# Stage borders of a two-block transformer kernel: row block 1 runs three tiles behind, splits and norms take another order

## The reference

```
first_block:                                   # once
    mixer: attention + hyena convolution + Fourier mixing, gated, w_out;  x = x + g1 * y
    x = x + g2 * expert_choice_moe(h2, ...)    # 16 experts, each takes 32 tokens
    return rms_norm(x, final_g)
second_block:  for i in range(2):              # two layers
    f = swiglu(rmsnorm(h, g[0]), gate[i,0], up[i,0], down[i,0]);  h = h + 0.5 * rmsnorm(f, g[1])
    mix = hybrid_mixer(rmsnorm(h, g[2]), rope tables, ...)        # latent + dilated attention
    h = h + rmsnorm(mix, g[3])
    f = swiglu(rmsnorm(h, g[4]), gate[i,1], up[i,1], down[i,1]);  h = h + 0.5 * rmsnorm(f, g[5])
    gate = sigmoid(rmsnorm(h, g[6]) @ w_ple_gate[i])
    h = h + rmsnorm((p[i] @ w_ple[i]) * gate, g[7])
```

## Time and profile before

| | |
|---|---|
| median of 3 runs | 2546.86 us (2542.1 to 2547.43) |
| profiled execution, time | 2549.01 us |
| profiled execution, span | 2547.7 us, mean granted clock 0.886 |
| TensorE busy | 2082.2 us (82%) |
| VectorE busy | 930.4 us (37%) |
| ScalarE busy | 603.8 us (24%) |
| memory read | 644.48 MB, mean 253 GB/s |

### The profile page before, as it was taken

The page is one execution under the profiler, slowest core; times in us unless marked ns, Lnnn a source line. Parts: engine busy times, 40 slices in busy tenths (PEclk is TensorE's granted clock), DMA queues, the critical chain, the costliest instruction groups (busy, mean ns, idle before and its releaser), DMA issues.

```text
span 2547.7 us, 28159 instructions
## 1 busy us (share of the span) xinstructions
PE 2082.2 (82%) x11876; PEld 1366.9 (54%) x11876; DVE 930.4 (37%) x1195; ACT 603.8 (24%) x744; POOL 68.8 (3%) x147
## 2 busy tenths in 40 slices
PE   6899998766666666666667999889997999889997
PEld 3556675211111111111115998678996998668995
DVE  1531323100000000000004666756656566756655
ACT  2121011000000000000002444344434444344443
POOL 0000000000000000000000000000001000000001
PEclk9898997977877777778787999989998999989998
DMA  7224454999999999999995554325553555305551
GB/s 304 102 106 179 167 215 184 425 424 425 425 424 425 424 425 425 424 425 425 424 425 233 190 187 139 120 77 180 191 188 118 179 193 176 120 33 191 192 192 64
DMA packets 93254, 647.37 MB, mean 254 GB/s; under 512 B 11495, under 2 KB 12424, under 8 KB 16328
## 3 DMA queue, kind: packets, MB, share of 16 engines
q1 hardware_dynamic: 89856, 639.93, 63.6%
q10 hardware_dynamic: 3272, 5.64, 0.6%
HBM read 644.48 MB, written 1.05 MB: 253 GB/s over the span
## 4 chain that ended last, share of the span: by engine, by line
PE 50%; DMA 33%; DVE 11%; ACT 3%; issue 2%; POOL 1%; SPq 1%; ACTq 0%; DVEq 0%; POOLq 0%
PE PS L812 10%; PE PS L814 10%; PE PS L813 10%; DMA ring<-in_md 9%; DMA ring<-in_mu 8%; PE PS L395 4%; DVE low L1589 3%; DMA XT<-in_mu 2%; DMA XT<-in_md 2%; PE PS L784 2%; PE PS L753 1%; DMA tables<-in_mu 1%; DMA QT<-in_mu 1%; DMA c_dft<-in_mu 1%; ACT WH L1942 1%
## 5 line engine op out<-in xcount | busy, mean ns | idle before, releaser
L1589 DVE TENSOR_TENSOR low<-ring,WH 128x2048 fp32r<-128x2048 f32 (+1 forms) x164 | 374.4, 2283 | 186.0 <-ACT WH L1942 183.4
L812 PE MATMUL PS<-XH,WH 128*128 128x256 f32 x1408 | 400.4, 284 | 17.0 <-DVE XL L1607 13.7
L813 PE MATMUL PS<-XL,WH 128*128 128x256 f32 x1408 | 399.1, 283 | 0.0
L814 PE MATMUL PS<-XH,low 128*128 128x256 f32 x1408 | 397.4, 282 | 0.0
L1942 ACT ACTIVATE WH<-ring 128x2048 fp32r<-128x2048 f32 (+1 forms) x164 | 313.0, 1909 | 33.2 <-PE PS L792 26.8
L812 PEld LDWEIGHTS PS<-XH,WH 128*128 128x128 f32 x1408 | 269.0, 191 | 19.6 <-issue 14.4
L814 PEld LDWEIGHTS PS<-XH,low 128*128 128x128 f32 x1408 | 271.4, 193 | 0.0
L813 PEld LDWEIGHTS PS<-XL,WH 128*128 128x128 f32 x1408 | 268.7, 191 | 1.4
L1571 DVE TENSOR_TENSOR SS<-SS,PS 128x512 f32<-128x512 f32 x16 | 11.0, 688 | 553.5 <-PE PS L753 553.5
L753 PE MATMUL PS<-ring,big 128*32 128x512 f32 x928 | 151.2, 752 | 74.8 <-DMA ring<-in_mu 45.2
L784 PE MATMUL PS<-ring,PT 128*32 128x512 f32 x480 | 98.4, 850 | 63.2 <-DMA ring<-in_md 53.0
(11 more groups left out here) (381 smaller groups left out, 2570.1 us busy)
## 6 DMA issues: line engine op xcount, KB each, us to landing
ring<-in_mu SPq DMA_DIRECT2D x62, 1024.0 KB, 26.6
ring<-in_md SPq DMA_DIRECT2D x60, 1024.0 KB, 26.7
ring<-in_mg SPq DMA_DIRECT2D x54, 1024.0 KB, 26.5
ring<-in_fg SPq DMA_DIRECT2D x44, 1024.0 KB, 4.8
ring<-in_fu SPq DMA_DIRECT2D x44, 1024.0 KB, 4.8
ring<-in_fd SPq DMA_DIRECT2D x44, 1024.0 KB, 4.8
ring<-in_wmod SPq DMA_DIRECT2D x24, 1024.0 KB, 6.9
XT<-in_mg SPq DMA_DIRECT2D x21, 1024.0 KB, 26.7
```

The costliest lines, as they stand in the source:

```text
L812: t.matmul(o, l[0], r[0], start=start, stop=False, skip_group_check=True)
L813: t.matmul(o, l[0], r[1], start=False, stop=False, skip_group_check=True)
L814: return t.matmul(o, l[1], r[0], start=False, stop=stop, skip_group_check=True)
L1589: own(v.tensor_tensor(low[:, w.slot.index, 0:size], w.flat, WH[:, w.slot.index, 0:size].bitcast(f32), ALU.subtract).then_inc(*c.wl.up()), ...
```

## The change

Eight parts:

1. *Entry.* The residual is added on TensorE: after expert 2, four identity matmuls add `XR` into the scatter banks. At the end VectorE and ScalarE copy two halves each. The splits of the first two tiles stand ahead of this, the third after the first gains. The loads of tiles 2 and 3 go ahead of the load of the gain row.
2. *Turn-overs* in expert 15: four identity matmuls after each of the 16 gate and up tiles, six after each of three down steps.
3. *Rope tables* made in block one, after the first affines; `pos` and `invs` are loaded early.
4. *Feed-forward end.* Down projections of tiles 8, 9 and 10 for m = 0, then 8 and 9 for m = 1, transposes of m = 0, then 10 for m = 1. The ring order of the tiles follows.
5. *Events 4l+1 and 4l+3.* Splits, norms, factors and gains of the two m take another order on VectorE, ScalarE and GpSimd; transposes of m = 1 lie between two halves of a weight block. The gate's sigmoid table is loaded early; event 4 of layer 0 handles m = 0 inside the gate's last block.
6. *Heads.* `latent_heads` alternates keys and queries; the second dilated rotation follows all copies on VectorE.
7. *Attention.* ScalarE copies probabilities at odd steps, VectorE at even ones.
8. *Event 4l+2.* TensorE's transposes of m = 1 stand before the last of the four `wple` groups.

```diff
 # queue
-                if n == 0 and f == 0:
+                if n == 1 and f == 0:
                     load_row(0, (c.scat, 16))
...
-                if n:
+                if 0 < n < 9:
                     load_split("fd", f * 11 + n - 1)
+                if n == 10:
+                    load_split("fd", f * 11 + 8)
+                    load_split("fd", f * 11 + 9)
+                if n == 11:
+                    load_split("fd", f * 11 + 10)
 # tensor_program
+                        if ex == 15:
+                            P.wait_ge(c.ht, 15)
+                            turn_over(2, 4)
...
+                    if ex == 15 and i < 3:
+                        P.wait_ge(c.pw, 16)
+                        turn_over(3, 6)
+                if ex == 2:
+                    P.wait_ge(c.xr, 4)
+                    for m in range(2):
+                        for n in range(2):
+                            t.matmul(PS[:, 4 + 2 * m + n, :], ident[:, :], XR[:, m, n * 512:n * 512 + 512],
+                                     start=False, stop=False, skip_group_check=True)
...
+                    if 0 < n < 9:
+                        whole_down(n - 1, 0)
+                        whole_down(n - 1, 1).then_inc(*c.wu.up())
+                    if n == 10:
+                        whole_down(8, 0)
+                        whole_down(9, 0)
+                    if n == 11:
+                        whole_down(10, 0).then_inc(*c.pj.up())
+
+                for n in (8, 9):
+                    whole_down(n, 1).then_inc(*c.wu.up())
                 added(event)
-                rows(0, 0, 0, XR, c.xs, 4 * event + 1)
-                down(10, 1, 1).then_inc(*c.wu.up())
-                rows(0, 1, 1, XR, c.xs, 4 * event + 2)
+                for j in range(2):
+                    rows(0, j, j, XR, c.xs, 4 * event + j + 1)
+                whole_down(10, 1).then_inc(*c.wu.up())
...
+                    for src, b0, j0 in ((KK, 2, 0), (QK2, 4, 0), (KK, 2, 2), (QK2, 4, 2)):
...
-                    held[2 + b] = [(c.pca if b else c.pcv, 8 + 6 * l + g // 2 + 1)]
+                    held[2 + b] = [(c.pcv if b else c.pca, 8 + 6 * l + g // 2 + 1)]
...
                         x.then_inc(*c.ple.up())
                         held[b] = [(c.em, c.ple.n)]
-                for j in range(2):
-                    rows(1, j, j, XR, c.xs, 4 * event + j + 3)
+                        if m == 1 and i == 0:
+                            for j in range(2):
+                                rows(1, j, j, XR, c.xs, 4 * event + j + 3)
...
 # vector_program, event 0
+            split_to(2)
             V.wait_ge(c.scat, 16)
             for m in range(2):
-                for j in range(2):
-                    h = slice(j * 512, j * 512 + 512)
-                    own(v.tensor_tensor(XR[:, m, h], XR[:, m, h], PS[:, 4 + 2 * m + j, :], ALU.add).then_inc(*c.xs.up()), c.xs)
-            split_to(1)
+                own(v.tensor_copy(XR[:, m, 0:512], PS[:, 4 + 2 * m, :]).then_inc(*c.xs.up(2)), c.xs)
...
 # vector_program, event 4l+1
+                add(0, acc(0), 0.5, 4 * l + 1, 22 * l + 9)
+                rows(0, 0, gT[:, g0 + 8:g0 + 16])
+                rows_factor(0)
+                split_to(tile("wid", 6 * l) + 1)
+                add(1, acc(1), 0.5, 4 * l + 1, 22 * l + 11)
+                split_to(tile("wid", 6 * l) + 2)
+                rows(1, 2, gT[:, g0 + 8:g0 + 16])
...
                 latent(0)
+                rows_factor(1)
+                dilated(0, 0, 6)
                 split_to(tile("wid", 6 * l) + 3)
-                dilated(0, 0, 6)
+                latent(1)
                 split_to(tile("wid", 6 * l) + 4)
-                latent(1)
...
-                    if g % 2:
+                    if g and g % 2 == 0:
...
-                        own(v.tensor_copy(PT2[:, 0, :], PS[:, 2, :]).then_inc(*c.pcv.up()), c.pcv)
+                        own(v.tensor_copy(PT2[:, 1, :], PS[:, 3, :]).then_inc(*c.pcv.up()), c.pcv)
...
 # vector_program, events 4l+3 and 4l+4
+                add(0, acc(0), 0.5, 4 * l + 3, 22 * l + 23)
+                rows(0, 0, gT[:, g0 + 24:g0 + 32])
+                gate_factor(0)
+                split_to(tile("wpg", 4 * l) + 3)
+                add(1, acc(1), 0.5, 4 * l + 3, 22 * l + 25)
+                split_to(tile("wpg", 4 * l) + 4)
+                rows(1, 2, gT[:, g0 + 24:g0 + 32])
+                gate_factor(1)
+                gated(0, 0)
+                gated(0, 1)
+                add(0, XN[:, 0, :], 1.0, 4 * l + 4)
```

More of the change, by code:

```diff
@@ L1126, in tensor_program @@
                         part(6 + n, 512, 1, j, "wpg", 4 * l + 2 * n + j)
+                        if l == 0 and n == 1 and j == 0:
+                            for h in range(2):
+                                rows(0, h, h, XR, c.xs, 4 * event + h + 1)
                 for b in range(4):
@@ L1927, in scalar_program @@
+                if l == 0:
+                    split_to(tile("fg", 22) + 1)
+                gated(1, 0)
+                if l == 0:
+                    rows(0, 0, gT[:, 40:48])
+                    w, s = factor(2)
+                    spread(0, w, s)
+                gated(1, 1)
+                add(1, XN[:, 1, :], 1.0, 4 * l + 4)
+                if l == 0:
+                    rows(1, 2, gT[:, 40:48])
+                    w, s = factor(3)
+                    spread(1, w, s)
         def scalar_program():
@@ L2222, in sum_square @@
                 own(square(src, col).then_inc(*c.sq.up()), c.sq)
+            A.wait_ge(c.dn, 64)
+            split_to(2)
             A.wait_ge(c.scat, 16)
[L2225 to L2226 removed]
+            for m in range(2):
+                own(copy(XR[:, m, 512:1024], PS[:, 5 + 2 * m, :]).then_inc(*c.xsa.up()), c.xsa)
             for m in range(2):
@@ new lines, in scalar_program @@
+                sum_square(acc(0), 0, *pj(l, 7))
+                split_to(tile("wpg", 4 * l) + 3)
+                own(a.activation(T1[:, 0:1], ident[:, 0:1], ACT.Sigmoid))
+                for j in range(2):
+                    rows(0, j, j)
+                sum_square(XR[:, 0, :], 2, c.xs, 4 * event + 2)
+                sum_square(acc(1), 1, c.wu, tile("fd", 22 * l + 21) + 1)
+                split_to(tile("wpg", 4 * l) + 4)
+                gate(0, 0)
+                for j in range(2):
+                    rows(1, j, 2 + j)
@@ new lines, in scalar_program @@
+                sum_square(XR[:, 1, :], 3, c.xs, 4 * event + 4)
+                gate(0, 1)
+                event = 4 * l + 4
+                sum_square(XN[:, 0, :], 0, c.gm, 4 * l + 2)
+                if l == 0:
+                    split_to(tile("fg", 22) + 1)
+                gate(1, 0)
+                if l == 0:
+                    for j in range(2):
+                        rows(0, j, j)
+                    sum_square(XR[:, 0, :], 2, c.xs, 4 * event + 2)
+                gate(1, 1)
+                sum_square(XN[:, 1, :], 1, c.gm, 4 * l + 4)
```

279 lines of the change are left out of this document (128 added, 151 removed).

## The result

The changed kernel takes 2500.66 us (median of 4, 2498.66 to 2504.43), the kernel before beside it 2544.48 (2537.21 to 2547.43): ratio 0.9834, 95% interval 0.9808 to 0.9859. That is 44 us or 1.7% faster, where 73 us were forecast. The sign and most of block two came as forecast. The time lies just inside the range of 2452 to 2502 and outside the likeliest case (2462 to 2486). But the forecast reckoned from 2546.86, and the kernel before beside this run had 2544.48: counted from there the range ends at 2499.6, and the time is 1 us beyond it.

The account below looks back on a forecast made before the run. Transfers bind block one's experts; block two's borders lose time to TensorE idling and low clock. 8.4 + 23.4 + 26 - 4.2 + 9.6 + 10.0 = 73.2 us saved, giving 2474 against the median; range 2452 to 2502.

Parts of the forecast that it names:

- likeliest case: The prediction's own case for the whole kernel: a time of 2462 to 2486 us, chance 0.48.
- Block one: Start to last scatter: rope tables fit into VectorE idle time, added matmuls hide behind transfers; no gain or loss.
- (a): Entry to block two: earlier splits and shared copies start the feed-forward sooner, rope tables leave it; 8.4 us gained.
- (b): Feed-forward to mixer, twice: reordered down projections, VectorE list and head transposes bring first scores 11.7 us earlier each, 23.4 together.
- (c): Attention, twice: probability copies no longer wait behind VectorE's splits, 55 us each; 14.5 and 11.5, together 26 us gained.
- (d): Mixer to feed-forward, twice: ScalarE's fourth group copy delays the high part, feed-forward 2.1 us later; a loss of 4.2 us.
- (e): Feed-forward to gate to next layer: earlier gate split removes the 4.55 us wait; next layer 9.6 us earlier.
- (f): The end, same gate without a next layer: its waits and cold tails go; 10.0 us gained.
- that rival (2480): Before the attention scores: transposes don't warm the clock, costing 6.4 us; total 2480, chance 0.08.
- The ring slots held longer: Block two's feed-forward ends: slots freed later make loads late, 20 us per border, 80 in all; 2554, chance 0.02.
- VectorE is late for half: Block two's tails: VectorE late for half of what (b), (e) and (f) free, 21.5 us; 2495, chance 0.12.
- Attention stays bound: Attention: VectorE or the clock still binds, so 26 us becomes 13.7; total 2486, chance 0.17.

Follow-up runs that it names:

- e1: The changed kernel with the two small rope-table loads issued near 33 us instead of ahead of ScalarE's first work: 2497.62 us, ratio 0.9812.
- e2: The changed kernel with TensorE's transposes of rows 128 to 255 at event 4l+2 behind the fourth embedding group again: 2493.63 us, ratio 0.9792.
- e3: The kernel before plus only the attention copies swapped (ScalarE at odd steps, VectorE at even ones): 2523.88 us, ratio 0.9913.
- e9: The changed kernel with 224 unused bytes per partition ahead of block one's tiles, restoring the old address remainders by 512: 2493.33 us, ratio 0.9806.
- e13: The changed kernel with VectorE's addition for rows 128 to 255 ahead of a weight tile's split at event 4l+1: 2503.33 us, ratio 0.9843.
- e6: The kernel before with 32 unused bytes ahead of block one's tiles and no instruction changed: 2555.04 us, ratio 1.0040.
- e12: The changed kernel with VectorE's second dilated rotation ahead of the four head copies instead of behind them: 2502.72 us, ratio 0.9831.

## Why the prediction was right or wrong, step by step

**Block one: the step that failed.** "In block one the rope tables fall into 8.35 us of VectorE idle before 52.23: 5.5 us fit, nothing; without that cover they cost up to 5.5, and the two small loads ahead of the first ScalarE work up to 2." The tables' work was indeed hidden. The loads cost 3.4 us (e1 against e2, the change against e3), since each issue took 1.6 and 2.8 us there. And the sum had no term for where the tables are kept: 6.4 us by e9. I had written of the transfer-bound experts "Nothing done to TensorE there is worth anything", and did not ask what else could change a transfer. Together 9.8 us. The remaining 1.7 of the 11.5 are what three differences leave: the kernel before's own profile reached the experts 3.4 us sooner than e3, which has the same instructions up to there; its experts were 0.9 shorter than e9's; and the last down group and the scatter took 2.5 less in the change, the scatter 3.70 instead of 5.5 (but 3.67 in e3 too, without turn-overs).

**(a) 8.4, measured 6.0.** The first matmul came 1.7 us earlier, not 4.4. The second split ended at 1379.1, 2 us after the scatter, and not ahead of its end; VectorE's copies and TensorE's wait of 2.82 us follow it. The third tile started 5.2 us earlier, not 7.6, for it carries the first matmul's shortfall of 2.7. The rope tables gave what they should.

**(b) 11.7 each, measured 9.9 and 9.4.** The waits of 3.19 and 2.54 us were to shrink to 1.5 and 1.3; they are 2.71 and 2.17. e13 shows why: VectorE's work in front of them is one serial list, and reordering it moves the wait. The head transposes went as forecast: forty in a row, at a granted clock of 1.00 from 1623.5 to 1629.0, then eight score matmuls in 1.13 us, where sixteen took 3.75. The rule on transposes from the Trainium skill (TensorE: Matmul & The Clock Gate, Part 4: PE-mode transpose) would have left the scores cold; they were not, so that rival (2480) is out. Whether transposes can raise the clock from the low level is not shown, since here it was high before them.

**(c) 26, measured 21.9.** The mechanism of the copies is confirmed by e3. Their price is less sure: 26.5 against the profile that I forecast from, 23 by the medians, 19.9 against e6. That profile had slow attentions, so part of my 26 was its luck. What was missing in the working is the moved rotation: counted as a gain in (b), as nothing in (c). e12 shows both sides.

**(d) -4.2, measured -6.5,** and 7.0 by e2. Right mechanism, undersized: besides the ScalarE order, the transposes wait 2.02 us for the addition, time that the fourth group used to fill.

**(e) 9.6, measured 10.8; (f) 10.0, measured 10.4.** Right. The 4.55 us wait at the gate is 0.8, the long chain of rows 128 to 255 remains as a wait of 4.05.

**The sum.** 73.2 less 9.8 (block one), less 11.3 (net shortfall of a to f), less 1.7: 50.4, the profiled difference. The medians give 43.8, as the profiled execution before was 4.5 us above its median and that of after 2.0 below.

**Rivals.** The ring slots held longer did not bite: no feed-forward end of block two waits for a transfer. "VectorE is late for half" of (b), (e) and (f) named the right engine, but 2.5 us are missing there and not 21.5. "Attention stays bound" allowed 13.7; it is 21.9.

## What to carry to other kernels

Where transfers bind, the addresses are part of the schedule: a new tile ahead of the landing buffers shifts them all. Put large landing buffers on multiples of 512 bytes (the best tried here), and check their addresses after every change to the allotment. A load that looks free by its size is priced by the queue it is issued in: issue small loads that are wanted late from an engine's first idle spell, not from its start-up list. When a piece of work is moved, book it in the stretch that receives it as well as in the one that loses it.

## What the runs showed of the hardware that was not expected

- 1 MB loads into 13 memories moved 421 GB/s with seven of them 32 bytes off a multiple of 64, 422 with these on multiples of 64, 425 with six of them on multiples of 128, 426 with all seven on multiples of 512, and 427 with the ring slots there too. The 16 experts took 933 to 934, 930 to 931, 926 to 927, 922, and 920 to 921 us.
- The issues of the same two small loads took 1.55 and 2.82 us on ScalarE's queue at 5 us, while SyncE issued its first eight weight loads, and 0.36 and 0.45 us at 31 us. What makes them slow is open. The other queue's traffic alone does not: the nine issues before them on ScalarE, from 0.71 us on beside the same loads of SyncE, took 0.41 to 0.65 us each. ScalarE's own loads that had not landed yet are as likely a cause; neither was tried by itself.
- After the same wait of TensorE of 2.7 us the clock stayed at 1.00 in one execution and averaged 0.89 in another; that makes 3 us at one place. The kernel before's attention, same instructions, took 64.6 us in one execution (clock 0.89) and 69.5 in another (0.83).
